# Loading expert weights in quads of chunks in place of pairs in the middle rounds

## What is computed

```python
def hierarchical_moe(x, g_ffn, w_rg, b_rg, w_re, b_re, w_gate, w_up, w_down):
    xn = rmsnorm(x, g_ffn).reshape(bsz * L, D_MODEL)
    ...
    for g in range(N_EXPERT_GROUPS):
        h = jax.nn.silu(jnp.einsum('nd,edf->nef', xn, w_gate[g])) * jnp.einsum('nd,edf->nef', xn, w_up[g])
        out = out + jnp.einsum('nef,efd->nd', h * combine[:, g, :, None], w_down[g])
    return x + out.reshape(bsz, L, D_MODEL)
```

## Time and profile before

| | |
|---|---|
| median of 3 runs | 1589.99 us (1589.52 to 1591.32) |
| the profiled execution | 1589.37 us |
| its span, first to last instruction | 1587.7 us |
| TensorE busy (PE) | 1374.1 us, 87% of the span |
| VectorE (DVE), ScalarE (ACT), GpSimd (POOL) busy | 556.2, 407.4, 20.4 us |
| read from memory | 540.30 MB, 343 GB/s over the span |
| granted TensorE clock, mean | 0.943 |

### The profile page before, as it was taken

How to read it: one execution, slowest core, us unless ns; L and a number is a source line. 1 busy time by engine, 2 the same in 40 slices (tenths; PEclk the granted TensorE clock), 3 DMA queues, 4 the chain that set the end, 5 groups by cost and what they waited for, 6 DMA issues and landing times.

```text
span 1587.7 us, 24107 instructions
## 1 busy us (share of the span) xinstructions
PE 1374.1 (87%) x9971; PEld 923.5 (58%) x9971; DVE 556.2 (35%) x898; ACT 407.4 (26%) x623; POOL 20.4 (1%) x54
## 2 busy tenths in 40 slices
PE   9999999999999999999778768778768767857866
PEld 8999999999999999962222322322312312412411
DVE  6657765554455555432112112112112111111114
ACT  6545343333333343331102002002002002002003
POOL 0000000000000000010000000000000000000000
PEclk9999999999999999999999889989889989889889
DMA  9777445545555769799999999999999999999997
GB/s 366 289 270 279 158 159 186 185 161 195 177 181 185 266 244 380 288 397 418 436 430 427 433 431 430 432 432 431 432 431 432 432 428 433 431 430 433 431 427 316
DMA packets 45017, 544.68 MB, mean 343 GB/s; under 512 B 6041, under 2 KB 8217, under 8 KB 13985
## 3 DMA queue, kind: packets, MB, share of 16 engines
q1 hardware_dynamic: 44680, 543.96, 84.1%
q10 hardware_dynamic: 288, 0.04, 0.0%
HBM read 540.30 MB, written 3.68 MB: 343 GB/s over the span
## 4 chain that ended last, share of the span: by engine, by line
PE 62%; DMA 36%; ACT 1%; issue 0%; DVE 0%; SPq 0%; POOL 0%; ACTq 0%; POOLq 0%; DVEq 0%
DMA ring<-in_expert_chunks 36%; PE bank L1630 12%; PE bank L1631 12%; PE bank L1632 12%; PE bank L2102 6%; PE bank L2099 5%; PE bank L2016 3%; PE bank L1957 1%; PE bank L2002 1%; PE bank L2008 1%; PE bank L1995 1%; ACT side L1064 1%; PE bank L1949 1%; PE bank L1889 1%; PE bank L1891 0%; PE bank L1890 0%
## 5 line engine op out<-in xcount | busy, mean ns | idle before, releaser
L1119 DVE TENSOR_TENSOR w_lo<-ring,w_hi 128x1024 fp32r<-128x1024 f32 x216 | 255.9, 1226 | 227.2 <-ACT w_hi L822 226.6
L1630 PE MATMUL bank<-xn_hi,w_hi 128*128 128x264 f32 x1120 | 318.9, 285 | 0.0
L1631 PE MATMUL bank<-xn_lo,w_hi 128*128 128x264 f32 x1120 | 317.3, 283 | 0.0
L1632 PE MATMUL bank<-xn_hi,w_lo 128*128 128x264 f32 x1120 | 317.1, 283 | 0.0
L822 ACT ACTIVATE w_hi<-ring 128x1024 fp32r<-128x1024 f32 x216 | 217.1, 1053 | 373.8 <-PE bank L1632 316.2
L2099 PE MATMUL bank<-side 128*32 128x512 f32 x1024 | 154.3, 743 | 100.8 <-DMA side<-in_expert_chunks 100.6
L1630 PEld LDWEIGHTS bank<-xn_hi,w_hi 128*128 128x128 f32 x1120 | 210.9, 188 | 1.5 <-issue 1.4
L1631 PEld LDWEIGHTS bank<-xn_lo,w_hi 128*128 128x128 f32 x1120 | 211.1, 188 | 0.1
L1632 PEld LDWEIGHTS bank<-xn_hi,w_lo 128*128 128x128 f32 x1120 | 210.0, 187 | 0.0
L2099 PE MATMUL bank<-ring,side 128*32 128x512 f32 x752 | 105.4, 684 | 54.7 <-DMA ring<-in_expert_chunks 54.7
L2099 PEld LDWEIGHTS bank<-side 128*32 128x32 f32 x1024 | 34.0, 129 | 193.6 <-DMA side<-in_expert_chunks 109.4
(11 more groups left out here) (333 smaller groups left out, 1586.2 us busy)
## 6 DMA issues: line engine op xcount, KB each, us to landing
ring<-in_expert_chunks SPq DMA_DIRECT2D x33, 4096.0 KB, 34.3
side<-in_expert_chunks SPq DMA_DIRECT2D x28, 4096.0 KB, 39.9
ring<-in_dense_units SPq DMA_DIRECT2D x108, 1024.0 KB, 4.8
trunk<-in_expert_chunks SPq DMA_DIRECT2D x13, 4096.0 KB, 43.8
ring<-in_expert_chunks SPq DMA_DIRECT2D x20, 2048.0 KB, 15.7
ring<-in_expert_chunks SPq DMA_DIRECT2D x17, 1024.0 KB, 19.2
side<-in_expert_chunks SPq DMA_DIRECT2D x5, 2048.0 KB, 10.9
trunk<-in_expert_chunks SPq DMA_DIRECT2D x5, 2048.0 KB, 18.3
```

The lines of the kernel that those rows point to most:

```text
L1119: V.tensor_tensor(w_lo[n % 2][:, js, :], raw[n % 2][:, js, :], w_hi[n % 2][:, js, :], ALU.subtract).then_inc(lo_done, 1)
L1630: mm(ps[:, 0:n], w_hi[b][:, j, :], x_hi[:, j, :], start=j == k0, stop=False)
L1631: mm(ps[:, 0:n], w_hi[b][:, j, :], x_lo[:, j, :], start=False, stop=False)
L1632: ins = mm(ps[:, 0:n], w_lo[b][:, j, :], x_hi[:, j, :], start=False, stop=j == k1 - 1)
```

## The change

The rounds 1 to 6 load pairs 5 and 6 as one transfer, pairs 7 and 8 as one, and of the next round pairs 0 and 1 as one and pairs 2 and 3 as one. Each is a quad: four chunks, 8 MB, with rows of 64 KB. The host packs the four chunks side by side, in the order in which the two places lie on chip. Pairs 4, 9, 10 and 11 stay as they are. For this the places 0 and 1 are made neighbours in `ring`, 3 and 4 in `side`, and the small tiles of the router that lay between them move elsewhere.

The quad's transfer signals `full` of its first pair's place; `full` of the second and both `second_in` are incremented when it is issued. The issues in the middle rounds become: the quad of pairs 5 and 6 after chunk 3, that of 7 and 8 after chunk 7, pair 9 after 9, 10 after 15, 11 after 17, the next round's quad of 0 and 1 after 17, its pair 4 after 19 and its quad of 2 and 3 after 23. Pairs of a quad that are loaded one by one (rounds 0 and 1, last round) are read as parts of the quad's rows.

```diff
+QUADS = {0: 0, 1: 0, 2: 4, 3: 4, 5: 10, 6: 10, 7: 14, 8: 14}
...
-        pair = [view(ring, 0, 2 * CHUNK), view(ring, UNIT0, 2 * CHUNK), view(trunk, 0, 2 * CHUNK),
-                view(side, 4096, 2 * CHUNK), view(side, 12544, 2 * CHUNK)]
+        pair = [view(ring, 0, 2 * CHUNK), view(ring, 2 * CHUNK, 2 * CHUNK), view(trunk, 0, 2 * CHUNK),
+                view(side, 4352, 2 * CHUNK), view(side, 12544, 2 * CHUNK)]
...
-        at = 2 * CHUNK
-        r1 = [view(ring, at + 3 * i, 3) for i in range(12)]
...
+        r1 = [view(small, 88 + 3 * i, 3) for i in range(12)]
+        thr = view(small, 124, 9)
+        thr2 = view(ring, 4 * CHUNK, 9)
+        npf = view(ring, 4 * CHUNK + 9, 2)
+        quad = {0: view(side, 4352, 4 * CHUNK), 2: view(ring, 0, 4 * CHUNK)}
+        quad[5], quad[7] = quad[0], quad[2]
+
+        at = 4096
         combx = view(side, at, 3, NX + EPR)
...
+            def quad_rows(c0):
+
+                return expert_chunks.rearrange("r c p n -> r (c p n)")[:, c0 * P * CHUNK:(c0 + 4) * P * CHUNK].rearrange(
+                    "r (p m) -> p r m", p=P)
...
+            def quad_after(q, p, base, of_round):
+
+                sp.wait_ge(e_used, base + (p + 1))
+                sp.sem_inc(second_in[q], 16)
+                sp.sem_inc(second_in[q + 1], 16)
+                sp.sem_inc(full[PAIR_SLOT[q + 1]], 16)
+                sp.dma_start(quad[q].rearrange("p (o n) -> p o n", o=1), quad_rows(QUADS[q])[:, of_round, :]).then_inc(full[PAIR_SLOT[q]], 16)
...
-                    for q in range(5, PAIRS):
+                    quad_after(5, 3, at, bass.ds(r, 1))
+                    quad_after(7, 7, at, bass.ds(r, 1))
+                    for q in (9, 10, 11):
                         pair_after(q, FREED_BY[q], at, bass.ds(r, 1))
-                    for q in range(5):
-                        pair_after(q, AHEAD[q], at, bass.ds(r + 1, 1))
+                    quad_after(0, 17, at, bass.ds(r + 1, 1))
+                    pair_after(4, 19, at, bass.ds(r + 1, 1))
+                    quad_after(2, 23, at, bass.ds(r + 1, 1))
```

More of the change, by code:

```diff
@@ L321, in branch_kernel @@
         at += CAP
-        assert at <= 4096 + 2 * KT * T
+        assert at <= 4352
         at = 12544 + 2 * CHUNK
@@ L538, in _, with pair_rows @@
                     unit_load(sp, bass.ds(g * 8 + (N_MKV + N_Z + u - 2), 1), u % 2)
+            def quad_rows(c0):
+                return expert_chunks.rearrange("r c p n -> r (c p n)")[:, c0 * P * CHUNK:(c0 + 4) * P * CHUNK].rearrange(
+                    "r (p m) -> p r m", p=P)
+            def pair_rows(q, round_of, n0=0, n1=2 * CHUNK):
+                if q in QUADS:
+                    off = 2 * CHUNK if PAIR_SLOT[q] in (1, 4) else 0
+                    return quad_rows(QUADS[q])[:, round_of, off + n0:off + n1]
+                return pair_v[:, q, round_of, n0:n1]
             def words_of(c, n0, n1, round_of, signal, first=False):
                 at = place(c)[1]
-                src = chunk_v[:, c, round_of, n0:n1] if c // 2 == PAIRS - 1 else pair_v[:, c // 2, round_of, at + n0:at + n1]
+                src = chunk_v[:, c, round_of, n0:n1] if c // 2 == PAIRS - 1 else pair_rows(c // 2, round_of, at + n0, at + n1)
                 sp.dma_start(words(c, n0, n1, first).rearrange("p (o n) -> p o n", o=1), src).then_inc(signal, 16)
@@ L547, in chunk_half @@
                 at = place(c)[1]
-                return pair_v[:, c // 2, 0:1, at + n0:at + n1]
+                return pair_rows(c // 2, slice(0, 1), at + n0, at + n1)
             def one_load(c, round_of, first=False):
@@ L569, in pair_load @@
                     sp.sem_inc(second_in[q], 16)
-                    sp.dma_start(pair[s].rearrange("p (o n) -> p o n", o=1), pair_v[:, q, round_of, :]).then_inc(full[s], 16)
+                    sp.dma_start(pair[s].rearrange("p (o n) -> p o n", o=1), pair_rows(q, round_of)).then_inc(full[s], 16)
                 else:
@@ L2139, in pack_experts @@
     for q in range(PAIRS - 1):
+        if q in QUADS:
+            continue
         order = slice(None, None, -1) if HIGH_FIRST[PAIR_SLOT[q]] else slice(None)
@@ L2142, in pack_experts @@
         out[:, 2 * q:2 * q + 2] = np.ascontiguousarray(both).reshape(ROUNDS, 2, P, CHUNK)
+    for c0 in sorted(set(QUADS.values())):
+        order = []
+        for q in sorted((c0 // 2, c0 // 2 + 1), key=lambda q: PAIR_SLOT[q]):
+            order += [2 * q + 1, 2 * q] if HIGH_FIRST[PAIR_SLOT[q]] else [2 * q, 2 * q + 1]
+        both = out[:, order].transpose(0, 2, 1, 3)
+        out[:, c0:c0 + 4] = np.ascontiguousarray(both).reshape(ROUNDS, 4, P, CHUNK)
     return out
```

## The result

The changed kernel takes 1603.03 us (median of 5 runs, 1602.64 to 1606.3) where the kernel before took 1589.74 us in the same session: ratio 1.0088, 95% interval 1.0077 to 1.01. It is slower by 13.3 us. That is the forecast's direction, but more than three times its size and outside its range. The profiled execution took 1602.73 us, its span is 1601.0 us.

What follows compares the result with a forecast made beforehand. The expert stage was taken as bound by its stream of bytes. +3.7 (quad of pairs 7 and 8) + 0.4 (pair 10) - 0.5 (rows) = +3.6, rounded to +4 us: 1594.0 us median, range 1588.2 to 1600, the forecast's own 1591 to 1598.

Steps and rivals of the forecast that it cites:

- What bounds the kernel: Expert stage: a stream of bytes at 431 GB/s; time is bytes by rate plus time the queue runs dry.
- Edit 2: Places in ring and side and the small router tiles move: nothing in time.
- rival (c): Quad reads: the rate falls with the 64 KB pitch, 1% or 5 us on top, about 1599 us; chance 3%.
- Edit 1: Rounds 1 to 6: 24 quads replace pairs, same bytes in longer rows; 0.5 us saved, between 0 and 2.2.
- Edit 4, the quad of pairs 7 and 8: Its issue after chunk 7, rounds 2 to 6: 0.75 us late each, 3.7 us in all, 0 to 8.5.
- The clock's price: TensorE after idle time: starts at half clock, losing 1.4 to 2.9 us, middle 2.1.
- The latency from issue to landing: A load issued into an empty queue: lands its transfer time plus 2.3 us later.
- Edit 4, pair 10: Its issue after chunk 15, only pair 9 queued: late by 0 to 0.4 us, six times; 0.4 in sum, at most 2.4.
- Edit 4, pair 11: Its issue after chunk 17: 17.3 to 18.8 us against 19.46 queued, covered by 0.7 to 2.2 us.
- issue delay plus latency under the queued time: Every issue: the stream stays whole if delay after the needed landing plus 2.3 us is under the queued time.
- (b): Quad of pairs 7 and 8 and pair 10 both late through long half clock: 14 us, 1600 to 1606; chance 9%.
- The signs named ahead: Expert stage profile: DMA share under 1.00, quad issue 17 to 19 us after landing, quad landings over 19.5 apart, first chunks 3.6.

Runs made afterwards that it cites:

- the run with the later quad: The changed kernel with the quad of pairs 7 and 8 issued after chunk 8 instead of chunk 7: 1614.85 us, ratio 1.0158.
- the layout alone: The changed kernel's packing and places, with all transfers and waits as in the kernel before: 1589.6 us, ratio 1.0.
- the clock held up: The changed kernel with identity matmuls in TensorE's idle time: 12 ahead of chunk 4 and 8 of chunk 14, 1606.48 us; or 15 ahead of chunk 4, 1600.01 us.
- the extra matmuls: The changed kernel with unused identity matmuls in TensorE's idle time, 12 ahead of chunk 4 and 8 ahead of chunk 14: 1606.48 us, ratio 1.0114.
- The extra matmuls ahead of chunk 4: The changed kernel with 15 unused identity matmuls ahead of the wait for chunk 4 only: 1600.01 us, ratio 1.007.

## Why the prediction was wrong

**What bounds the kernel** held. The stream is the bound, and time in which the queue is empty comes back in the total: in the run with the later quad five delays of 2.4 us cost 11.8 us.

**Edit 2** held, and rival (c), the pitch of 64 KB, is out: the layout alone is at 1.0.

**Edit 1** was undersized and harmless. 0.5 us were taken for the longer rows; the packets show 1.9.

**Edit 4, the quad of pairs 7 and 8.** The mechanism, the place and the number of rounds were right. The term was 0.75 us for each, and measured 1.3 to 2.0. Its parts: 15.8 us at full clock was right (15.9 with the clock held up). The clock's price was taken as the middle of 1.4 to 2.9, 2.1, and was 2.4. The queued time was 19.35 and not 19.46. The latency from issue to landing was 40.1 - 18.2 - 19.35 = 2.55 us (chunk 4 to chunk 14, 1041.49 to 1081.59) and not 2.3. None is far off, but the term is a small difference of large ones: 0.3, 0.1 and 0.25 us nearly double it. Over five rounds the quads cost 8.3 us where 3.7 stood, 4.6 us of the miss. (The upper end of 1.7 us is a slip: its own terms, 18.7 + 2.3 - 19.46, give 1.5, and three of the five gaps are at or above that 1.7.)

**Edit 4, pair 10,** is the step that failed. Its range was 8.6 to 10.1 against 9.73 us, and it was priced as a rare loss of 0.07 us a round, with 2.4 us in sum as the most. In the changed kernel TensorE idles 9.43 us ahead of chunk 14 (8.6 to 9.6 in the six rounds) and then runs at half clock for 5.6 us; in the kernel before the same spot had 2.47 us of idle time ahead and was back at full clock by chunk 15. The upper end of the clock's price was the usual case and not the worst, since the change itself makes the idle times long. The 4.9 us at full clock was about right (5.1 with the clock held up), and so the issue stood at the very end of the range, 7.8 us. With the latency of 2.6 us in place of 2.3, 7.8 + 2.6 - 9.7 is 0.7 us, and the packets show 0.7 to 1.4: 6.1 us in sum where 0.4 stood and 2.4 was the most, so 5.7 us of the miss. What lies above 0.9 is in rounds 1, 2 and 5, in which the last engines finish pair 10 over 1 us behind the first; why isn't known.

**Edit 4, pair 11,** was called covered by 0.7 us at the least. It lost 1.7 us in sum, though it was issued 3.4 us and more before the queue ran out. The rule "issue delay plus latency under the queued time" says that nothing is lost there, so the rule is incomplete; what it lacks stays open.

**The end** was left out. The prediction followed the queue only and not what TensorE has still to do when the last quad lands: chunks 4 to 23 of the last round. 1.0 us.

**The rivals.** (b), both margins fail, is what happened. It was priced at 14 us and 1600 to 1606 us, for the right reason (long half clock, pair 10 about 1 us late in six rounds), and was given 9%. The forecast and the range treated two terms as independent that hang on one cause: if chunks after a quad start at half clock, both are late in every round.

**The signs named ahead** came as said: a DMA share under 1.00, the issue 18.2 us after the landing, chunk 14 40.1 us after chunk 4 where two quads take 38.7, and 3.64 us for the first chunk of a quad.

## What to carry to other kernels

In a stream that is bound by transfers, a larger transfer is paid in issue lead: list for every issue what is still queued when its place comes free, and ask for some 4 us more than the compute ahead of it needs (pair 11 lost next to nothing from 3.8 us on, and pair 10 nothing at 4.2 with the extra matmuls), at the clock that the engine will have after the idle time that the change itself makes. Where two such margins hang on one cause, price them together and for every round. And look who ends last in the last round: work that waits under a long transfer can't be hidden behind a stream that is over.

## What was not expected of the hardware

- A queue that was refilled less than about 2 us before it ran out lost the difference, whichever transfer it was. By the last engine, lead and loss add up to 1.9 to 2.4 us in twelve of the fifteen gaps of pair 10 and the quad that were set out above, and to at most 3.3 in the others; by the mean of the 16 engines it is 1.8 to 2.1 in all of them. The extra matmuls ahead of chunk 4 gave exceptions: 2.7 to 3.0 us of lead and 0.7 to 2.3 lost. Part of the loss is the wait for the first packet, which started 0.96 to 0.98 us after the issue at each of the five late quads. The first packets after the gap are slow as well: an engine's first 64 KB packet took 2.4 to 3.4 us, mostly about 3, where 2.42 is usual.
- A row of 64 KB moves as one packet of 2.42 us, one of 32 KB takes 1.215. A quad so takes 19.35 us and two pairs take 19.43: the last doubling was worth 0.4%.
- After idle times of the same length TensorE began at either clock. With the extra matmuls a chunk took 3.57 us (half clock) after 2.56 us of idle time and 1.92 us (full clock) after 2.52; in a later round of that trace it took 3.45 us after 2.50 us and 1.92 after 2.79. After 0.23 us it stayed at full clock.
